# One block from attention to experts, and expert rows spread over the slots by a fixed order

## The reference, cut to what matters

```
def hier_moe(x, p):
    l1 = (x @ p['w_router1']).astype(jnp.float32) + p['b_router1']
    top1_p, grp = lax.top_k(jax.nn.softmax(l1, axis=-1), 1)
    ...
    top_v, top_i = lax.top_k(l2, TOP_K_INNER)
    top_w = jax.nn.softmax(top_v, axis=-1) * top1_p
    ...
        hg = jnp.einsum('nd,edf->nef', x, p['w_gate'][gi])
        hu = jnp.einsum('nd,edf->nef', x, p['w_up'][gi])
        h = jax.nn.silu(hg) * hu * combine[:, gi, :, None]
        y = y + jnp.einsum('nef,efd->nd', h, p['w_down'][gi])
```

## Time and profile before

| what | value |
|---|---|
| median of 3 runs | 1089.39 us |
| the profiled execution's own time | 1084.67 us |
| its span, first to last instruction | 1082.8 us |
| mean granted clock of TensorE | 0.944 |
| busy: PE, DVE, ACT, POOL | 84%, 30%, 18%, 10% |
| moved by DMA | 273.11 MB, 252 GB/s over the span |

### The profile page before, as it was taken

One profiled execution on the slowest core, in us unless ns is written; L12 is line 12 of the kernel. 1 busy time (PEld: TensorE's weight loads), 2 busy tenths in 40 slices (PEclk: granted clock), 3 DMA queues, 4 the chain that ended last, 5 costly groups with the idle time before them and its releaser, 6 DMA issues. The chain is left out here.

```text
span 1082.8 us, 13539 instructions
## 1 busy us (share of the span) xinstructions
PE 914.3 (84%) x5419; PEld 498.4 (46%) x5419; DVE 323.4 (30%) x697; ACT 192.9 (18%) x462; POOL 112.7 (10%) x131
## 2 busy tenths in 40 slices
PE   4899969999967787889997999989888777787774
PEld 2455535565536453444554555545434333343332
DVE  3333252323244477864534111111111111111110
ACT  1121121112102467561100010000000000000000
POOL 0000124122000000000000021111110110110111
PEclk9999988999979797889998899989999999999998
DMA  9753017495306100004929699999999999999991
GB/s 390 312 189 108 15 55 179 110 220 134 119 1 209 74 1 1 1 1 196 354 101 414 264 414 415 408 415 415 412 421 415 411 417 410 410 416 412 409 386 54
DMA packets 66055, 273.11 MB, mean 252 GB/s; under 512 B 11760, under 2 KB 27951, under 8 KB 40575
## 3 DMA queue, kind: packets, MB, share of 16 engines
q1 hardware_dynamic: 52215, 255.18, 60.2%
q0 software_dynamic: 7376, 12.85, 4.3%
q10 hardware_dynamic: 6400, 4.20, 1.6%
HBM read 265.64 MB, written 19.10 MB: 263 GB/s over the span
## 5 line engine op out<-in xcount | busy, mean ns | idle before, releaser
L2144 PE MATMUL ps<-room 128*64 128x256 f32 x800 | 98.0, 392 | 32.7 <-DMA room<-in_w_up 19.7
L2144 PEld LDWEIGHTS ps<-room 128*64 128x64 f32 x800 | 56.5, 140 | 70.7 <-DMA room<-in_w_up 29.0
L2144 PE MATMUL ps<-w_a,room 128*64 128x256 f32 x576 | 70.4, 394 | 18.9 <-DMA w_a<-in_w_up 10.7
L2144 PE MATMUL ps<-w_b,room 128*64 128x256 f32 x576 | 67.6, 383 | 19.4 <-DMA w_b<-in_w_up 10.8
L441 PE MATMUL ps<-w_b,room 128*128 128x454 f32 (+1 forms) x240 | 80.9, 548 | 0.7 <-ACT room L414 0.7
L2055 POOL DMA_INDIRECT out_y<-room,halves x32 | 50.1, 1565 | 290.9 <-ACT room L2326 290.9
L2326 ACT ACTIVATE room<-ps,slot_w 128x512 f32<-128x512 f32 x32 | 22.0, 687 | 283.6 <-PE ps L2171 283.6
L2144 PEld LDWEIGHTS ps<-w_a,room 128*64 128x64 f32 x576 | 41.4, 141 | 45.3 <-DMA w_a<-in_w_up 15.2
L890 PE MATMUL ps<-room,w_a 128*128 128x378 f32 x192 | 62.0, 482 | 0.0
L2144 PEld LDWEIGHTS ps<-w_b,room 128*64 128x64 f32 x576 | 40.2, 137 | 43.9 <-DMA w_b<-in_w_up 15.3
L2236 DVE SCALAR_TENSOR_TENSOR room<-room,ps 128x256 f32<-128x256 f32 x32 | 13.5, 421 | 155.3 <-ACT room L2320 155.3
(11 more groups left out here) (356 smaller groups left out, 1204.4 us busy)
## 6 DMA issues: line engine op xcount, KB each, us to landing
room<-in_w_down SPq DMA_DIRECT2D x26, 1024.0 KB, 28.8
room<-in_w_gate SPq DMA_DIRECT2D x25, 1024.0 KB, 28.0
room<-in_w_up SPq DMA_DIRECT2D x25, 1024.0 KB, 29.0
w_a<-in_w_gate SPq DMA_DIRECT2D x18, 1024.0 KB, 27.6
w_a<-in_w_up SPq DMA_DIRECT2D x18, 1024.0 KB, 27.8
w_a<-in_w_down SPq DMA_DIRECT2D x18, 1024.0 KB, 29.3
w_b<-in_w_gate SPq DMA_DIRECT2D x18, 1024.0 KB, 28.3
w_b<-in_w_up SPq DMA_DIRECT2D x18, 1024.0 KB, 28.6
```

Of the source, the lines that this page charges most:

```text
L2144: ins = nc.tensor.matmul(ps[h * CAP:h * CAP + CAP, bank, 0:FH], xT[:, n // 2 % 2, k, CAP * slot:CAP * slot + CAP], w[k // 4][:, k % 4, h * ...
```

## The change

It has two parts. The blocks `attend_and_mix` and `experts` become one block: `experts` no longer opens its own block but returns its five functions, and each engine runs them right behind those of `mix`. The drain, the wait for all engines and the clearing of semaphores between the two are gone. Two instructions of VectorE that had no semaphore of their own now get one (`ch.then`).

The second part is a new row of constants, `C_SLOT`, which takes the place of 0 to 63 in the comparison that makes `slot_hot`. A pair of rank r no longer goes to slot r but to slot 8 (r mod 8) + (r div 8 + 4 ((r mod 8) div 2 mod 2)) mod 8. Ranks 0 to 7 so take the slots 0, 8, 20, 28, 32, 40, 52, 60, the next eight ranks the slots one higher, and so on: the first 32 ranks fill slots 0-3, 8-11, 20-23, 28-31, 32-35, 40-43, 52-55 and 60-63. The load of constants grows from 1153 to 1217 columns.

```
-CW = C_LAST + 1
+C_SLOT = C_LAST + 1
+CW = C_SLOT + CAP
...
+    rank = np.arange(CAP)
+    c[:, C_SLOT + rank % 8 * 8 + (rank // 8 + 4 * (rank % 8 // 2 % 2)) % 8] = rank
...
             nc.vector.tensor_tensor(slot_hot, rank.unsqueeze(2).broadcast_to([P, 2 * NT, CAP]),
-                                    self.c(C_EI, CAP).unsqueeze(1).broadcast_to([P, 2 * NT, CAP]), ALU.is_equal).then_inc(hot_ready, 1)
+                                    self.c(C_SLOT, CAP).unsqueeze(1).broadcast_to([P, 2 * NT, CAP]), ALU.is_equal).then_inc(hot_ready, 1)
...
-            nc.vector.tensor_copy(self.n_over[:, :], f(60, 1)[0:1, 0, :])
+            ch.then(nc.vector.tensor_copy(self.n_over[:, :], f(60, 1)[0:1, 0, :]))
             dve.wait_ge(w_table_in_psum, 1)
-            nc.vector.tensor_scalar(self.slot_w[:, 0:NEXP], ps[:, 1, 0:NEXP], 0.5, None, ALU.mult)
+            ch.then(nc.vector.tensor_scalar(self.slot_w[:, 0:NEXP], ps[:, 1, 0:NEXP], 0.5, None, ALU.mult))
...
-    def attend_and_mix(self):
+    def attend_to_experts(self):
...
+        st_e, experts = self.experts()
-        with self.nc.Block("attend_and_mix") as block:
+        with self.nc.Block("attend_to_experts") as block:
...
                 mix[4](pe, attend[4](pe))
+                experts[4](pe)
         st_a.close()
-        self.close(st_m)
+        st_m.close()
+        self.close(st_e)
```

More of the change, by code:

```diff
@@ L1965, in _ @@
                 mix[0](sp)
+                experts[0](sp)
             @block.gpsimd
@@ L1970, in _ @@
                 mix[1](pool)
+                experts[1](pool)
             @block.vector
@@ L1974, in _ @@
                 mix[2](dve, attend[2](dve))
+                experts[2](dve)
             @block.scalar
@@ L1979, in _ @@
                 mix[3](act)
+                experts[3](act)
             @block.tensor
@@ L2057, in scatter, with sync @@
                                     compute_op=ALU.add).then_inc(sem, 16)
-        block = st.enter_context(nc.Block("experts"))
-        @block.sync
-        def _(sp):
+        def sync(sp):
             again = [3 * n + m + RING for n, m in uses[:24]]
@@ L2082, in _, with gpsimd @@
                     sp.dma_start(self.w_a[:, 2 * UNIT:3 * UNIT].rearrange("p (h j d) -> p h j d", h=2, d=D), vd[bass.ds(e, 1), :, :, :, :].rearrange("e p h j d -> (e p) h j d")).then_inc(o_w_in, 16)
-        @block.gpsimd
-        def _(pool):
+        def gpsimd(pool):
             pool.wait_ge(x_turned, 2)
@@ L2114, in _, with tensor @@
                     pool.sem_inc(tile_free, 1)
-        @block.tensor
-        def _(pe):
+        def tensor(pe):
             def turn(out, rows, chunks):
@@ L2221, in _, with vector @@
                     ins.then_inc(o_y_psum, 1)
-        @block.vector
-        def _(dve):
+        def vector(dve):
             ch = Chain(dve, steps)
@@ L2288, in _ @@
                 ch.then(nc.vector.tensor_tensor(o_slot_hot, slot.unsqueeze(2).broadcast_to([P, 2 * NT, CAP]),
-                                                self.c(C_EI, CAP).unsqueeze(1).broadcast_to([P, 2 * NT, CAP]), ALU.is_equal))
+                                                self.c(C_SLOT, CAP).unsqueeze(1).broadcast_to([P, 2 * NT, CAP]), ALU.is_equal))
                 hot, weighted = o_tile_hot[:, :, 0, :], o_tile_hot[:, :, 1, :]
@@ L2312, in _, with scalar @@
                     nc.vector.tensor_copy(hT[:, :, :].rearrange("p k s -> p (k s)"), ps[:, 5, 0:KF * CAP]).then_inc(o_hT, 1)
-        @block.scalar
-        def _(act):
+        def scalar(act):
             def tanh(n):
@@ L2340, in _ @@
                     nc.scalar.activation(yb[:, 0, :], ps[:, 6, :], ACT.Copy, scale=self.slot_w[:, bass.ds(j + NEXP, 1)]).then_inc(o_y_ready, 1)
-        self.close(st)
+        return st, (sync, gpsimd, vector, scalar, tensor)
     def run(self):
@@ L2389, in run @@
             self.project_and_stream(ExitStack())
-            self.attend_and_mix()
-            self.experts()
+            self.attend_to_experts()
 def kernel(**inputs):
```

## The result

The changed kernel takes 1100.94 us (median of 4 runs, 1099.98 to 1102.36) against 1086.56 us of the kernel before beside it: ratio **1.0124**, 95% interval 1.0091 to 1.0158. It is slower by about 1.2%, some 13.5 us. The forecast was +4.7 us and 1094; the range to 1103 holds the time, but the sum was some 9 us short of the change. The profiled execution took 1099.98 us, its span is 15.1 us longer than that of before. Four marks in the timelines of the two kernels say where: the first gather of the seam, the first load issued after it, the start of the last half of the last up product, and the end of the span.

What follows compares the result with a forecast made beforehand. The prediction took the experts' weight loads, paced by the slowest of sixteen DMA engines, as the bound. Seam -5.6, slots +9.9 and last scatter +0.4 gave +4.7 us, 1094 us against the median; range 1079 to 1103.

Steps and rivals of the forecast that it cites:

- Seam, -5.6 forecast: Between attention and experts: no drain and partly a faster clock bring the first load earlier, -5.6 us, between -3.9 and -6.4.
- Rival (d): At the seam: the first gather lands as late as the second did, so the seam gives about -2; 1098 us, chance 0.05.
- Which engine has which slots: Gathers and scatters: an engine serves four neighbouring slots and the four 32 higher; the new order gives the busiest 71 more packets.
- Rival (a): Experts' slots: another pairing or larger groups let the new order even the engines out; 1076 us, chance 0.09.
- Rival (b): Experts' stage: the new slots cost nothing because loads wait elsewhere; -5.6 us, 1084 us, chance 0.1.
- The price, "I take 0.14, nearer to the second": Experts' stage: each extra data packet on the busiest engine costs 0.14 us, so 71 cost +9.9 us, between +8.7 and +13.0.
- the 0.183 of the queue's share: Experts' stage: POOL's queue time, 474 us, over some 2,585 packets gives 0.183 us each, empties counted in.
- a half-empty end "for some 20 us or more": When loads run out: DMA share falls to about a half for some 20 us or more, half the engines done early.
- The end, +0.4: Last scatter: it ends after seven data packets of an engine in place of four, +0.4 us.
- The wider constants, 0: Load of constants: 64 more columns, 32 KB, cost 0 to 0.2 us, taken as 0.
- rival (c): Experts' stage and seam: packets on busy engines cost more and the clock falls before gate; +9.5 us, 1099 us, chance 0.18.

Runs made afterwards that it cites:

- e1_seam: The changed kernel with the first slots again, so the one block alone is tested; ratio 0.9954 to the kernel before, stage 456.43 us.
- e3_moved: The changed kernel with the slots of the second half of the partitions moved on by 16; ratio 0.9911 to the kernel before, stage 450.12 us.
- e2_slots: The kernel before, still two blocks, with the new order of slots alone; ratio 1.0163 to the kernel before, stage 471.48 us.
- e9_onegroup: The changed kernel with each expert's first eight rows on one pair of engines, the others dealt evenly over seven pairs; ratio 1.0164 to the kernel before.
- e6_plain: The changed kernel with scatters that write rows without adding to y; ratio 0.9917 to the kernel before, stage 453.10 us.

## Why the prediction was right or wrong, point by point

**Seam, -5.6 forecast: right.** -5.75 measured, -5.5 in e1_seam. The drain was the wait, and the turns ran at the upper clock. That the sum is so close is in part luck. The wait gave 4.57 us where 3.9 were forecast, and the clock gave 1.2 where 1.7 were: gate had the upper level for the first 0.5 us only and took 3.27 us from its start, 598.81, to the load's issue, against 3.72 and 1.98, a quarter of the difference and not half. Rival (d) fell: the first gather carries more data on fewer engines, but the turns start 8.39 us after its issue, within the 8.6 us of before.

**Which engine has which slots: right.** Eight engines with data and 72 small packets, a DMA share of a half at the end, and e3_moved. Rival (a) is out, and turned into the version that is faster. Rival (b) is out by e2_slots.

**The price, "I take 0.14, nearer to the second": wrong.** This step failed. The slots cost 14 to 15 us, not 9.9. I had two sources and chose the lower, the lead of the other engines when the loads run out (0.124), because it is a difference between engines. But that lead was over one pair at the top (252 and 248 packets, the next engine 224), and this pair stands closer to the others than its count says: in the last load's completions the third engine is 1.5 us ahead of it, where 28 packets at 0.16 would make 4.5. So 9.2 us divided by 74 packets came out too low. The price between kernels is 0.155 to 0.161 us, nearer to the 0.183 of the queue's share. 71 x 0.16 makes 11.4 us. The other 3 us are those by which the kernel before lies below the line of the others. A likely reading is that its top pair, like that of e9_onegroup, holds no engine that is late for another reason, while eight engines at 305 to 323 do. That is inferred and not shown; the runs show one late engine at 344 packets directly, at 252 only a stage 3 us below the line. The cause of this part stays open.

The forecast's other sign, a half-empty end "for some 20 us or more", came as some 15. A smaller error of the same kind: an engine's lead can't grow for ever. In the sixteen completions of the last load, e9_onegroup's fourteen light engines are all 18 to 20 us ahead, where 170 packets at 0.16 would be 27; before, the two lightest stood 20 us ahead, not 25. There are only so many loads issued, and an engine that has done them all waits. In the changed kernel the light eight reach a lead of 21 to 24 us near 792, and keep about 20 from there on.

**The end, +0.4: too low.** It is +2.3. I priced the last scatter's own packets and missed that it now waits for the one before to land, which makes it 1.0 us later (the wait of 4.14 us is ended by the DMA; e2_slots has the same, 3.85 us, and e1_seam ends it on ScalarE, 3.16). The other 1.4 us lie between the last scatter's issue and the span's end, 11.22 us in place of 9.85; 0.6 of them e1_seam has too, with the old slots (10.42).

**The wider constants, 0: open**, as told above.

The outcome is the size that rival (c) names, over 0.20 us a packet and 1% slower, but not by its mechanism. The seam lost 0.5 us more to the clock than the forecast had counted, no more. And the traces show no weights held up behind an adding packet. The 8 KB packets take 0.309 us at the median of the records and under 0.325 at 95% of them, before and after. The changed kernel has more long ones, over 0.4 us, but they don't come with the adding packets: 14 of 7,970 from 615 to 780 us, beside 656 adding packets; 268 of 11,960 from 780 to 1040, when the light engines have run as far ahead as they can; none of 399 from 1060 on, when only the busy eight have loads left, beside 56 adding ones. In e6_plain, which adds nothing, there are 155 of 19,554 from 640 to 1040. It fits that they are packets of light engines that start again after a wait; which engine a packet belongs to the records don't say.

## What to carry to other kernels

When sixteen engines share every load, count the small packets by engine, and compare the busiest before with the busiest after: here an order that looks even (eight slots apart) put 323 on eight engines, and moving half of it by 16 slots put 186 at most on any and turned 1.2% slower into 0.9% faster. Price a packet from two kernels or from its own records, not from how far engines have drifted apart in one, since the drift is bounded by what has been issued, and an engine can be late for another reason. And a block's end may cost a drain that waits for a transfer nobody needs yet: 5.5 us here at the first load's issue, about a fifth of it by the clock.

## What the runs showed of the hardware that I had not expected

- A 2 KB row that is added costs an engine 0.176 us in the records, more than a 4 KB row that is gathered (0.16); written plainly it takes 0.085, or half of a joined 4 KB packet.
- An index out of bounds costs next to nothing: 0.009 us in the records for an empty, and 216 of them in place of data gave back 34.7 us.
- Two engines at 344 packets end the stage at 473.2 us, four at 479.0, with the same longest list on one engine; all engines but one are done by 475.0, and that one is 4 us late.
- With the clock kept at 1.00 in the first gate, SyncE issues the first load 0.87 us sooner, and the last up half starts no sooner: 465.0 us after the first gather in both kernels.
